# A hybrid decoder layer on one core: the down passes' splitting in larger pieces, and ScalarE further ahead

## The reference

```python
top_s, pos = lax.top_k(cand_s, PEER_TOPK)            # 8 heads, 16 experts for each head
gate = jax.nn.softmax(top_s, axis=-1)
act = jax.nn.gelu(jnp.einsum('cd,chkd->chk', hc, expert_u[idx]))
return jnp.einsum('chk,chkd->cd', gate * act, expert_v[idx])
```

## Time and profile before

| | |
|---|---|
| three runs | 2219.4 us median, 2213.34 to 2234.45 |
| the profiled execution | 2225.7 us, of which the span is 2224.0 |
| mean granted TensorE clock | 0.993 |
| busy | PE 98%, DVE 75%, ACT 55%, POOL 31% |
| the down passes | 1556.2 to 2207.1 us of the span |

### The profile page before, as it was taken

One profiled execution on the slowest core, in us unless ns is written; L12 is line 12 of the kernel. 1 busy time (PEld: TensorE's weight loads), 2 busy tenths in 40 slices (PEclk: granted clock), 3 DMA queues, 4 the chain that ended last, 5 costly groups with the idle time before them and its releaser, 6 DMA issues.

```text
span 2224.0 us, 55792 instructions
## 1 busy us (share of the span) xinstructions
PE 2187.3 (98%) x16578; PEld 2140.6 (96%) x16578; DVE 1663.1 (75%) x3039; ACT 1215.7 (55%) x2217; POOL 691.6 (31%) x516
## 2 busy tenths in 40 slices
PE   9999999999999999999999999999999998999997
PEld 8999899999999999999999999999999998999997
DVE  8777788887766667888885444476788886888887
ACT  6445366667455445555555544455555654655664
POOL 0221100002011000788888888300623233111120
PEclk9999999999999999999999999999999999999999
DMA  7887756666556556887876888698889988899985
GB/s 240 283 294 235 240 188 211 200 214 220 183 184 209 170 168 183 189 180 186 188 179 168 208 186 182 174 336 266 252 275 325 335 298 281 267 291 299 299 282 184
DMA packets 337993, 514.36 MB, mean 231 GB/s; under 512 B 87276, under 2 KB 126564, under 8 KB 337772
## 3 DMA queue, kind: packets, MB, share of 16 engines
q1 hardware_dynamic: 263244, 427.59, 61.2%
q0 software_dynamic: 58016, 71.54, 12.8%
q10 hardware_dynamic: 16640, 14.16, 2.0%
HBM read 487.87 MB, written 25.24 MB: 231 GB/s over the span
## 4 chain that ended last, share of the span: by engine, by line
PE 73%; DMA 2%; DVE 1%; issue 1%; ACT 0%; DVEq 0%; ACTq 0%; SPq 0%
PE ps L2167 17%; PE ps L314 15%; PE ps L317 15%; PE ps L313 15%; PE ps L2171 9%; DMA gat<-expert_v,gidx 1%; DVE lo L301 0%; DMA raw<-expert_v 0%; PE ps L2191 0%; PE ps L1394 0%; DVE gacc L2033 0%; ACT hi L296 0%; DVE x L2148 0%; PE ps L2200 0%; DVE fin_r L374 0%
## 5 line engine op out<-in xcount | busy, mean ns | idle before, releaser
L301 DVE TENSOR_TENSOR lo<-raw,hi 128x512 fp32r<-128x512 f32 x1504 | 1024.8, 694 | 458.5 <-ACT hi L296 432.9
L296 ACT CAST hi<-raw 128x512 fp32r<-128x512 f32 x1504 | 924.6, 620 | 731.8 <-PE ps L317 441.5
L313 PE MATMUL ps<-h_hi,hi 128*128 128x264 f32 (+1 forms) x3200 | 822.3, 286 | 1.4 <-DVE h_lo L950 1.4
L314 PE MATMUL ps<-h_lo,hi 128*128 128x264 f32 (+1 forms) x3200 | 821.0, 286 | 0.0
L313 PEld LDWEIGHTS ps<-h_hi,hi 128*128 128x128 f32 x3200 | 602.5, 188 | 8.4 <-issue 5.7
L314 PEld LDWEIGHTS ps<-h_lo,hi 128*128 128x128 f32 x3200 | 602.8, 188 | 0.0
L317 PE MATMUL ps<-h_hi,lo 128*128 128x264 f32 (+1 forms) x3200 | 523.9, 285 | 6.0 <-DVE lo L301 5.9
L1726 POOL DMA_INDIRECT w_spill<-chosen,widx x256 | 438.5, 1713 | 268.4 <-DVE widx L1949 188.8
L2167 PE MATMUL ps<-whl,hi 128*128 128x432 f32 x2048 | 491.0, 362 | 1.8 <-ACT half_sum L1810 1.2
L317 PEld LDWEIGHTS ps<-h_hi,lo 128*128 128x128 f32 x3200 | 444.7, 188 | 8.1 <-DVE lo L301 8.1
L2167 PEld LDWEIGHTS ps<-whl,hi 128*128 128x128 f32 x2048 | 349.6, 191 | 10.7 <-issue 1.6
(11 more groups left out here) (302 smaller groups left out, 1724.9 us busy)
## 6 DMA issues: line engine op xcount, KB each, us to landing
raw<-u_tiles SPq DMA_DIRECT2D x512, 256.0 KB, 3.1
raw<-expert_v SPq DMA_DIRECT2D x512, 256.0 KB, 5.9
raw<-weights SPq DMA_DIRECT2D x480, 256.0 KB, 3.3
w_spill<-zeros ACTq DMA_DIRECT2D x16, 864.0 KB, 6.1
wld<-w_spill SPq DMA_DIRECT2D x32, 432.0 KB, 4.4
qb<-q_spill POOLq DMA_DIRECT2D x8, 512.0 KB, 6.2
w_spill<-chosen,widx POOLq DMA_INDIRECT x256
u_spill<-ust SPq DMA_DIRECT2D x128, 24.0 KB
```

The source lines that it names most:

```text
L296: nc.scalar.copy(hi[k % SPLIT][:], raw_quarter(k)).then_inc(hi_done, 1)
L301: nc.vector.tensor_tensor(lo[k % SPLIT][:], raw_quarter(k), hi[k % SPLIT][:].bitcast(F32), ALU.subtract).then_inc(lo_done, 1)
L313: pe.matmul(out, a, rhs[0][:, first + j, 0:n], start=start and j == 0, stop=False)
L314: pe.matmul(out, a, rhs[1][:, first + j, 0:n], start=False, stop=False)
```

## The change

It concerns the down passes alone; the order of TensorE's, GpSimd's and SyncE's work stays.

- VectorE's split takes a whole half (1024 elements a partition) in one instruction. It waits for both quarters' rounded parts and for the place of both, and counts `lo_done` up by two. In half c it splits half c+1, that is the quarters 2c+2 and 2c+3.
- `hi` gets eight places: the four of before and four in `hi_more`, where places 1 and 2 of `wld` and a strip behind them were. ScalarE's cast of a quarter waits until TensorE is done with the quarter eight before it.
- In half c ScalarE casts the quarters 2c+5 and 2c+6 (FAR = 5) instead of 2c+3 and 2c+4. Two more casts stand ahead of the loop, two fewer in it. `w_part` stays behind the casts of its half.
- The ring `raw` and the four places for `lo` stay as they are.
- The factors of `times_up` in the down pass come to a place of their own, `wlast`, and SyncE doesn't wait for `w_mul` before the first of these loads.

The core of the diff:

```diff
-    hi = [place(f"hi{s}", at["raw"] + 2048 * s, [P, QT, P], F32R) for s in range(SPLIT)]
-    lo = [place(f"lo{s}", at["hi3"] + 2048 * s, [P, QT, P], F32R) for s in range(SPLIT)]
+    hi_all = place("hi", at["raw"], [P, SPLIT * QT, P], F32R)
+    lo_all = place("lo", at["hi"], [P, SPLIT * QT, P], F32R)
...
+    hi_more = place("hi_more", more, [P, SPLIT * QT, P], F32R)
+    hi8 = hi + [hi_more[:, QT * s:QT * s + QT] for s in range(SPLIT)]
+    hi_pair = [(hi_all if s < 2 else hi_more)[:, HALF * (s % 2):HALF * (s % 2) + HALF] for s in range(4)]
+    lo_pair = [lo_all[:, HALF * s:HALF * s + HALF] for s in range(2)]
...
         def half(p, i, k, last=2):
             c = NK * p + 8 * i + k
-            for r in range(last):
-                split(eng, C0 * 2 + 2 * (c - k), 2 * k + AHEAD + r)
-            if k % 2 == 0 and last == 2:
+            split(c, k)
+            if k % 2 == 0 and not (isinstance(c, int) and c + 2 >= 2 * NK):
                 w_part(c + 2, p, i, k + 2)
             between(p, i, k)
...
-        sp.wait_ge(w_mul, UP_CHUNKS + 1)
-        cells_in(UP_CHUNKS, 1)
+        cells_in(UP_CHUNKS, 3)
...
+        def split_far(q0, k):
+            act.wait_ge(raw_in[k // 2 % RAW][k % 2], 2 * q0 + 16 * (k // (2 * RAW)) + 16)
+            act.wait_ge(mm_done, q0 + k + 1 - SPLIT)
+            nc.scalar.copy(hi8[k % (2 * SPLIT)][:], raw_quarter(k)).then_inc(hi_done, 1)
...
+        def split(c, k):
+            for r in range(2):
+                if not (isinstance(c, int) and 2 * c + FAR + r >= 4 * NK):
+                    split_far(2 * C0 + 2 * (c - k), 2 * k + FAR + r)
...
+        def split(c, k):
+            if isinstance(c, int) and c + 1 >= 2 * NK:
+                return
+            q0, k = 2 * C0 + 2 * (c - k), k + 1
+            dve.wait_ge(hi_done, q0 + 2 * k + 2 * RAW + 2)
+            dve.wait_ge(mm_done, q0 + 2 * k + 2)
+            nc.vector.tensor_tensor(lo_pair[k % 2][:], raw[:, k % RAW], hi_pair[k % 4][:].bitcast(F32),
+                                    ALU.subtract).then_inc(lo_done, 2)
```

More of the change, by code:

```diff
@@ L202, in program @@
     wld = place("wld", at["W"], [P, 3, 4, TD])
-    gacc = place("gacc", at["wld"], [P, len(GROUPS), HALF * P])
+    more = at["W"] + 16 * TD
+    assert more + 8192 >= at["wld"]
+    gacc = place("gacc", more + 8192, [P, len(GROUPS), HALF * P])
     gat2 = place("gat2", at["gacc"], [P, HALF * P])
@@ L1532, in program @@
     route, route_seen = sem("route"), sem("route_seen")
-    u_out, w_in, w_mul = [sem("u_out0"), sem("u_out1")], [sem(f"w_in{h}") for h in range(3)], sem("w_mul")
+    u_out, w_in, w_mul = [sem("u_out0"), sem("u_out1")], [sem(f"w_in{h}") for h in range(4)], sem("w_mul")
     soft, soft_act, widx_made = sem("soft"), sem("soft_act"), sem("widx_made")
@@ L1609, in halves @@
                 for k in range(8):
[L1610 to L1613, removed]
+                    half(p, i, k)
             after_pass(p)
@@ L1626, in cells_in @@
         def cells_in(m, h):
[L1627 removed]
+            sp.dma_start(wld[:, h] if h < 3 else wlast[:], w_dram[bass.ds(4 * m, 4)].rearrange("n p t -> p n t")).then_inc(w_in[h], 16)
         def u_tiles_in(first, last):
@@ L1822, in between @@
                 scaled(k)
-        halves(act, w_part, split_hi, between, after_pass)
+        def split(c, k):
+            for r in range(2):
+                if not (isinstance(c, int) and 2 * c + FAR + r >= 4 * NK):
+                    split_far(2 * C0 + 2 * (c - k), 2 * k + FAR + r)
+        for k in range(AHEAD, FAR):
+            if k < SPLIT:
+                split_hi(act, 2 * C0, k)
+            else:
+                split_far(2 * C0, k)
+        halves(act, split, w_part, between, after_pass)
         nc.scalar.activation(gw[:, 0:2], eps[:], ACT.Sqrt)
@@ L2020, in times_up @@
             wv = W[:, bass.ds(4 * m, 4), :]
-            nc.vector.tensor_tensor(wv, wv, wld[:, h], ALU.mult).then_inc(w_mul, 1)
+            nc.vector.tensor_tensor(wv, wv, wld[:, h] if h < 3 else wlast[:], ALU.mult).then_inc(w_mul, 1)
         def w_part(c, p, i, k):
@@ L2137, in experts_vector @@
                     weighed(i, k // 2)
-        for k in range(8):
+        for k in range(7):
             split_lo(dve, 8 * (PAIR_U - 1), AHEAD + k)
@@ L2142, in experts_vector @@
         w_part(0, 0, 0, 0)
-        halves(dve, w_part, split_lo, between, after_pass)
+        def split(c, k):
[6 more added lines that the diff above has]
+                                    ALU.subtract).then_inc(lo_done, 2)
+        halves(dve, split, w_part, between, after_pass)
         dve_rstd(dve, LIVE, fin_r[:, 0], fin_r[:, 1], fin_r[:, 2], 4, D, 0, bank(0))
```

19 lines of the change are left out of this document (12 added, 7 removed).

## The result

| | us, median (lowest to highest) | ratio to the kernel before, 95% interval |
|---|---|---|
| before | 2222.3 (2213.3 to 2234.5), 6 runs | |
| changed | 2331.4 (2322.0 to 2335.4), 6 runs | 1.0487 [1.0451, 1.0522] |
| forecast | 2280 (2238 to 2320) | |

Slower, as forecast, but by 109 us instead of 54 to 60. The profiled execution of the changed kernel took 2334.8 us, its span 2332.7. In it raw loads are L296, ScalarE's casts L1787 and its copy of the weight pair L1782, VectorE's part of that pair L2048, the add L2054, the pair split L2171, TensorE's products L2197 (hi) and L2201 (lo), the row sum L2221, the gathers L1592.

The account below looks back on a forecast made before the run. The prediction took TensorE's matmuls as the bound, with 16.5 us lost in the down passes. Adding 31 us in pass 0 and 37 in pass 1, less 14 of old losses, gave +54 on 2225.7: 2280 us, range 2238 to 2320.

Parts of the forecast that it names:

- (a): VectorE's splits: one of 1024 takes 1.22 us against 1.38 for two, saving 41 us beside matmuls, worth nothing by itself.
- (b): VectorE's pair split after the add of gathered rows: 0.5 us less room than before.
- (c): ScalarE's weight-pair copy stands behind the cast of quarter 2c+6, which waits for raw data; VectorE and TensorE wait in turn.
- (d): SyncE's raw loads: four in a row after the pairs, the first some 0.2 us after its quarter is free, others 0.69 apart.
- (e): The fourth place for factors, the dropped w_mul wait and the moved buffers: off the path, costing nothing.
- The formula, s + s' = L - 4.10: Successive periods' lateness s and s', from load issue-to-landing time L: each period with an add grows by (L-4.10)/2 on average.
- Pass 1: Second down pass, three adds in four periods: late by 1.3, nothing and 1.0; 2.3 us 16 times, 37 us.
- L = 5.4: Issue-to-landing time of raw loads, in us, taken from the median in 1800:1890, the stretch judged nearest.
- The rule of the Trainium skill: HBM reads at large power-of-two row pitches are slow, so L would not fall as the kernel slows: 2318 us.
- The old losses of 16.5 us go except some 2.6: -14: Down passes: gathers get about half a microsecond more per period, so old losses go except the handover between passes.
- The landing did not hide it: Rival: loads land within 4.1 us of issue, so ScalarE's copy is in time; 2205 to 2240 us, chance 0.17.
- The clock fell: Rival: TensorE's pauses in nearly every period lower its clock to 0.94, costing 32 us; 2290 to 2350, chance 0.07.

Follow-up runs that it names:

- e9: The changed kernel with adds of gathered rows moved from even to odd halves and ScalarE's weight copy ahead of its two casts: 2219.4 us, 1.0013 times the kernel before.
- e4: The changed kernel with pair splits kept, but ScalarE at the four places and cast distance of the kernel before: 2298.0 us, 1.0179 times the kernel before.
- e1: The changed kernel with ScalarE's copy of the weight pair ahead of its two casts, on another chip: 2277.0 us, 1.0084 times the kernel before.
- e14: The changed kernel with ScalarE's weight copy ahead of its two casts, on a chip without the other chip's pause: 2253.4 us, 1.0131 times the kernel before.
- e3: The changed kernel with eight places and casts five ahead kept, but VectorE splitting by quarters in the old order: 2292.8 us, 1.0164 times the kernel before.
- e5: The changed kernel with the down passes' raw loads reading expert_u's tiles, each in one block, instead of expert_v: 2278.0 us, 1.0236 times the kernel before.
- e13: The changed kernel with raw loads from expert_u's tiles and three gathers in place of 96: 2215.8 us, 0.9981 times the kernel before.
- a_again: The changed kernel unaltered, run once more as reference: 2331.3 us, 1.0487 times the kernel before.
- e6: The changed kernel with three gathers in place of 96, raw loads keeping their source: 2284.7 us, 1.0278 times the kernel before.
- e8: The changed kernel with adds of gathered rows moved from even to odd halves, behind that half's pair split: 2342.5 us, 1.0562 times the kernel before.
- e12: The changed kernel with each gather of pass 0 held back until the first pair split behind the add ends: 2348.1 us, 1.0568 times the kernel before.
- e7: The changed kernel with VectorE splitting by quarters as before and ScalarE's weight copy ahead of its two casts: 2219.8 us, 1.0003 times the kernel before.

## Why the prediction was off by half

- **(a) The pair split costs 1.22 us**: right (1218 and 1220 ns measured). That its 41 us are worth nothing by themselves: right, e9 has the pairs and ends at 1.001.
- **(b) 0.5 us less room after the add**: right in direction, but I did not see what the pair does to the ring. It moves the split of 2c-4 behind the add. e4 prices this at 1.018 with near casts, where I had counted nothing.
- **(c) ScalarE's copy behind a far cast, that cast behind raw data**: right, step by step in the timeline. Taken away from the change it is the largest part (e1, e14); put in alone (e3, 1.016) it costs no more than the pair alone (e4, 1.018).
- **(d) The burst of four loads, 0.7 apart**: right (four in 2.41 us).
- **(e) Nothing for the fourth place of factors**: its stretch was not singled out. The first 15 periods lose 4 us in all.
- **The formula, s + s' = L - 4.10**: right in form, as the table above shows, but its constant has a slip. From the copy's end at T+L-1.80, the terms 0.52, 1.20 and 1.22 add up to T+L+1.14, not 1.19, and they leave out the 0.27 us from the copy's end to VectorE's start (1755.15 to 1755.42 in the earlier trace rows). The pair is due at T+4.90+0.44 = T+5.34, not 5.29. Together that is L - 3.93, and s of 1.09 where the table has 1.00 and the trace 1.16. It would have put some 10 us on the forecast.
- **Pass 1**: the pattern was right (a late period, one of 4.91, a late one, one of 4.91), and both late periods were forecast too short, at 1.3 and 1.0 us more than 4.9 where the trace has about 1.7 in each. L for 2c+6 was 5.7 there; by the formula as it stands that makes 46 us in place of 37, and 54 were measured. So L is about half of this error; the slip in the constant is most of the rest.
- **"L = 5.4"** is the step that failed. I took the median that the view gave for 1800:1890, because I reasoned that L falls when TensorE pauses. The figure was wrong, and the fall is small. In that view only the loads of one of the eight quarter places had a landing time, 7 of the 59, and that place's loads land earliest. Over all eight places, from the last arrival of each load, the median of 1800:1890 was 6.4, and that of 1640:1800 was 6.6, where the earlier trace rows have 5.4 and 6.3. The slower kernel got only slightly faster loads: over all eight places the median went from 6.6 to 6.2 in 1640:1800, with 261 GB/s instead of 322, and from 6.2 to 5.6 in 1900:2200. For 2c+6 L is 6.1 in pass 0. With it the formula gives 44 us for the 44 periods with adds ahead of the handover; measured were 45 more than before, and 50 more than 44 periods of 4.90.
- **The rule of the Trainium skill** that I weighed ("DMA: Bandwidth & Descriptors", section "Latency and other measured facts": reads of HBM at a row pitch of large powers of two are slow) gave 2318, and was nearer than my own choice. e5 and e13 against a_again and e6 show that the source counts, by 0.7 us of L beside gathers and 1.8 without them. Whether it is the power of two, or any pitch that long, no run here tells.
- **"The old losses of 16.5 us go except some 2.6: -14"** failed as well, and by as much. The handover between the passes got worse. VectorE gets a gathered row late, the pair is behind that add, and TensorE waits 3.09 us just ahead of the row sum:

```profile
1923.98 1.28 DVE L2054 SCALAR_TENSOR_TENSOR gacc<-gat,gw,gacc 128x1024 f32<-128x1024 f32 x1 [2.99 <-DMA gat<-expert_v,gidx]
...
1926.46 0.70 PE L2201 MATMUL ps<-whl,lo 128*128 128x216 f32 x4 [3.09 <-DVE lo L2171]
...
1928.70 6.88 PE L2221 MATMUL ps<-same,gacc 128*128 128x32 f32 x32
...
1935.42 1.79 PE L2197 MATMUL ps<-whl,hi_more 128*128 128x432 f32 x4
```

  The row sum took 3.60 us before and takes 6.88, and four products 1.79 instead of 0.95: the granted clock of 1920:1945 is 0.73. In e13, which has no such pause, that whole period is 8.5 us instead of 17.7. With the upper L alone (2318) the forecast would still have been 13 us short; with this term at nil as well it would have been 2332. That would have been luck in part, since 6.3 and 5.9 are above the 6.1 and 5.7 measured for 2c+6, and the constant errs the other way.
- **The rivals.** The landing did not hide it. The clock fell at the handover, for a moment near 2000 (0.72 in 1998:2004) and at the end (0.79 in 2300:2316), and stayed at 1.00 in 1640:1800 through 22 pauses of 0.3 us or more, none over 1.22. In e8, with pauses of 0.8 to 2.7 us, it was 0.95 there. By the Trainium skill's section "HAM oscillation — how this bites in real kernels" ("TensorE: Matmul & The Clock Gate") a kernel that waits in each round is throttled in each; the waits of the kernel described there are about 3 to 5 us. In the change, with shorter ones, the trace does not show it. The gathers came in time in all periods but one, at the end of pass 0.

## What to carry to other kernels

Before an instruction is placed behind a further one in an in-order engine, follow the loop to its end: which load feeds that one, which split frees its place, and what work of the other engine lies between the thing now delayed and that split. The slack of a loop is a length (here 4.1 us of landing time for a period of 4.9), and a larger instruction can move a release across a long neighbour without taking any longer itself. When a forecast hangs on one latency, count how many transfers are behind the median that a view shows, and take it from a stretch with the same neighbours in flight, not the same idle time.

## What the runs showed of the hardware

- **A gather's issue on GpSimd ends 0.8 us after VectorE's two-input subtract beside it.** Beside quarter splits of 0.69 us the gather (L1581 before) takes 1.14 us, beside pairs 1.68. In both it starts 0.35 us after the first split and ends 0.8 us after that split does. In e12, where it starts 0.86 us into a pair, it takes 1.18 and again ends 0.8 us after it. This is so for most gathers; 5 of 96 before and 11 of 96 in e7 took over 3 us, beside several quarter splits in a row. From the timelines of before and of the change:

```profile
1757.49 1.14 POOL L1581 DMA_INDIRECT gat<-expert_v,gidx  x1 [3.78 <-DVE gacc L2033]
```
```profile
1759.47 1.67 POOL L1592 DMA_INDIRECT gat<-expert_v,gidx  x1 [5.08 <-DVE gacc L2054]
```

  The first split before ends at 1757.13 + 0.69 = 1757.82 and the gather at 1758.63; after, 1759.12 + 1.22 = 1760.34 and 1761.14. The Trainium skill ("SBUF — State Buffer", section "Who interferes with whom") has a rule for it: a VectorE instruction with two inputs in SBUF contends with a GpSimd instruction that reads SBUF. The times agree with it; that this is the cause was not shown. In the change it cost next to nothing, since all gathers but one were in time.
- **The landing time of a load depended more on its company and its source than on the rate.** 3.2 us at 220 GB/s (e13), 5.0 at 198 GB/s (e6), 6.1 at 262 GB/s (a_again): the slowest stream of the three is not the one with the fastest landing.
- **A gather held back lengthens the loads that it then meets.** In e12, L of the later two loads of each burst rose to 6.66 and that of the earlier two fell to 4.8 to 5.3, with the same transfers in all.
